# Three taps of a depthwise convolution moved from TensorE to VectorE

## The chip, the cores and the metric

One core of a Trainium2 chip runs the kernel. The metric is the time on the device in microseconds, the median of several runs. A profile is taken of one execution; its span is the time from the first to the last instruction.

## The reference, cut to what matters

The model is a block of 272 tokens (16 meta tokens and 256 of the sequence) and then two blocks of 256 tokens with a width of 1024. The second of the three holds the mixer that the change touches. Its input projection gives `u_val` and `u_gate` of 512 channels each, and queries, keys and values of 8 heads. The two parts are computed beside each other:

```python
def causal_depthwise_conv(x, w):          # y_t = sum_j w_j * x_{t-W+1+j}
    ...
def conformer_conv(u_val, u_gate, conv_w, ln_g, ln_b):
    z = u_val * jax.nn.sigmoid(u_gate)
    z = causal_depthwise_conv(z, conv_w)   # W = 31, 512 channels
    z = layernorm(z, ln_g, ln_b)           # over the 512 channels
    return jax.nn.silu(z)

def mixer_ab(h, w_in, conv_w, ln_g, ln_b, w_out):
    ...
    ya = conformer_conv(u_val, u_gate, conv_w, ln_g, ln_b)
    yb = moba_attention(...)               # 8 heads, 256 tokens
    return jnp.concatenate([ya, yb], axis=-1) @ w_out
```

Everything is float32. Each weight matrix is multiplied in three passes of a high and a low part.

## The kernel before

Activations lie with channels on the 128 partitions and tokens along the free dimension. Weights stream from HBM in 281 slabs of 128x1024 through four buffers. SyncE loads a slab (`raw`), ScalarE makes the high part (`whi`, L464), VectorE subtracts for the low part (`wlo`, L839), and TensorE does the three products (`three`, L1236 to L1238). A `column` makes 128 output channels out of one slab, 24 matmuls of 256 columns; a `row` adds one slab's part to eight accumulators. VectorE's `take` (L883) moves a finished column from PSUM to `proj`, scales it, and then does the split of the slab three places ahead.

The order of work is written out by hand. In the mixer of the second block each engine runs a loop over the steps u = 0 to 18, and each engine's list for a step is executed in order; engines meet at semaphores only. On TensorE (the last loop of the printed code) a step holds: scores and transposes (even u) or attention products (odd u); then a weight column, if u is in `IN2_STEP`, whose keys are 1, 2, 3, 4, 6, 7, 8, 10 and 11; then for u = 1 to 8 half a convolution block (`conv_half`, block (u-1)//2, first half at odd u, second at even u); then at u = 9 the sum for the layernorm mean (L1618), at u = 10 that for the variance (L1623). Steps 5 and 9 hold no column.

The convolution. The 512 channels are four blocks of 128 in the order `GLU_ORDER`, and each block is four groups of 32 channels. GpSimd multiplies value and gate into `zpad` (30 zeros in front) and issues DMAs that lay four versions of each group, shifted by 0 to 3 tokens, on the 4 x 32 partitions of `zsh`. One matmul with a 128x32 matrix of diagonals then adds four taps of one group; eight of these (q = 0 to 7, `CONV_Q`) make the 31 taps and one of weight zero. A block is 8 x 4 matmuls into one half of the PSUM bank `acc_bank[3]`, and a half block is 16. With the last one `conv_summed` is raised. ScalarE then copies the block from PSUM to `cv` (L711, at even u, the last thing of the step but the layernorm) and raises `conv`. TensorE's first half of block i waits for `conv` >= i, and the mean's matmuls wait for `conv` >= 4.

VectorE's list for an even step: `maxima` (bias and maximum of the scores, L1089 and L899), `take` and split. For an odd step: `normalized` (reciprocal L905 and two scalings L908, which wait for ScalarE's exponentials), then `take` and split, if the step has a column. At u = 9 it also subtracts the mean (L1114).

The parameters that are per channel are packed in one tensor `par` of 144 columns, which ScalarE's queue loads first in the kernel. The third block's mixer has a convolution of 4 taps whose last three are chained VectorE instructions (L1191), each with its weight out of `par`.

Of the kernel before, what the change touches and what calls it, by code (L numbers as in the profile page):

```python
# [27 lines left out]
ALU = mybir.AluOpType  # L28
ACT = mybir.ActivationFunctionType
# [4 lines left out]
KC = DM // P  # L34
SEQ = 256
# [11 lines left out]
CONV_T = 31  # L47
CONV_C = 4
SHIFTS = 4
CONV_Q = 8  # L50
CONV_X = SEQ + SHIFTS * (CONV_Q - 1)
LRU_T = 4
LRU_C = 8.0
# [35 lines left out]
def in1_lo(d):  # L89
# [16 lines left out]
GLU_ORDER = (0, 2, 1, 3)  # L106
# [31 lines left out]
PAR = (("norm1", KC), ("norm2", KC), ("final_norm", KC), ("mix_norm_2", 2 * KC), ("mlp_norm_2", 2 * KC),  # L138
       ("final_norm_2", KC), ("c_conv_b_2", KC), ("c_b_r_2", KC), ("c_b_i_2", KC), ("c_lambda_2", KC),
       ("pool_scale", 2), ("fox_out_gain", 3), ("sb_out_gain", 3), ("ab_ln_g_2", CONV_C), ("ab_ln_b_2", CONV_C),  # L140
       ("c_conv_w_2", LRU_T * KC))
COL = {name: sum(n for _, n in PAR[:i]) for i, (name, _) in enumerate(PAR)}
PAR_N = sum(n for _, n in PAR)
G_PROD = PAR_N
# [22 lines left out]
def build(nc, slabs, xT, par_in, fbias_in, poolw_in, gatew_in, convw_in, out):  # L167
    with ExitStack() as ctx:
# [8 lines left out]
        acc_bank = bank[2:6]  # L177
# [4 lines left out]
        def half(b, j):  # L182

            return b[:, SEQ * (j % 2):SEQ * (j % 2) + SEQ]
# [28 lines left out]
        par = sb("par", [P, PAR_N + KC])  # L213
# [21 lines left out]
        zpad = sb("zpad", [P, CONV_C, CONV_X + SHIFTS])  # L235
        t8 = sb("t8", [P, KC, SEQ])
        cv = t8[:, 0:CONV_C, :]
# [6 lines left out]
        zsh = shared[:, n_convw:n_convw + n_zsh].rearrange("p (k g x) -> p k g x", k=CONV_C, g=4)  # L244
# [52 lines left out]
        conv_summed, conv = sem("conv_summed"), sem("conv")  # L297
# [145 lines left out]
        def _(act):  # L443
# [111 lines left out]
            for i in range(PIECES):  # L555
                act.wait_ge(x_loaded[i], 16)
                for k in (2 * i, 2 * i + 1):
                    g = GAIN[N_NORM1] + k
# [120 lines left out]
            for i in range(len(IN2_FIRST)):  # L679
                split_ahead(IN2 + i)  # L680
                if i in (1, 3, 5, 7):
                    k = GLU_ORDER[i // 2]
# [4 lines left out]
            for u in range(MOBA_U + 3):  # L687
                if u in IN2_STEP or u in OUT2_STEP:
                    split_ahead(n)
                    n += 1  # L690
                if u == max(IN2_STEP) + 1:
                    act.wait_ge(slab_used, OUT2)
                    operand_hi(A_CAT2, F_CAT2, CAT2_STEP[u])
                if u % 2 == 0:
                    if 1 <= u // 2 <= MOBA_S:
                        transposed(u // 2 - 1, FOX_S, moba_copies)
                    if u % 4 == 0 and u < MOBA_U:
                        pair = u // 4
                        act.wait_ge(vT, 7 + pair)
                        act.activation(vtok[:, 0:2, P * pair:P * pair + P],  # L700
                                       acc_bank[2][:, 0:2 * P].rearrange("p (g d) -> p g d", g=2), ACT.Copy).then_inc(v_ready, 1)
                    if u // 2 < MOBA_S:
                        probabilities(u // 2, FOX_S, MOBA_N)
                if u >= 6 and u % 4 == 2:
                    pair = u // 4 - 1
                    act.wait_ge(o_ready, FOX_S + 2 * pair + 2)
                    act.activation(af[:, PAIR_CHUNK[pair], :], aux_bank[:, 0:SEQ], ACT.Copy).then_inc(af_ready, 1)
                if 2 <= u <= 2 * CONV_C and u % 2 == 0:
                    i = u // 2 - 1
                    act.wait_ge(conv_summed, i + 1)  # L710
                    act.activation(cv[:, GLU_ORDER[i], :], half(acc_bank[3], i), ACT.Copy).then_inc(conv, 1)  # L711
                if u == LN_MEAN_STEP:
                    for k in range(CONV_C):
                        act.wait_ge(ln_dev, k + 1)
                        act.activation(sq[:, k, NMETA:], cv[:, k, :], ACT.Square).then_inc(ln_sq, 1)
                if u == LN_VAR_STEP:
                    act.wait_ge(ln_var, 1)
                    inverse_root(r1[:, :], std[:, NMETA:], half(acc_bank[3], 1), CONV_C * P).then_inc(ln_std, 1)
                if u == MOBA_U:
                    for k in range(CONV_C):  # L720
                        g, b = COL["ab_ln_g_2"] + k, COL["ab_ln_b_2"] + k
                        act.wait_ge(ln_norm, k + 1)
                        act.activation(af[:, CONV_CHUNK + k, :], cv[:, k, :], ACT.Silu, scale=par[:, g:g + 1], bias=par[:, b:b + 1])\
                            .then_inc(af_ready, 1)
                if u in CAT2_STEP and u > max(IN2_STEP) + 1:
                    operand_hi(A_CAT2, F_CAT2, CAT2_STEP[u])
# [57 lines left out]
            for i in range(2 * KC):  # L784
                if IN3 + i < OUT3 - 1:
                    split_ahead(IN3 + i)
                if i < KC:
                    w, b = COL["c_conv_w_2"] + KC * (LRU_T - 1) + i, COL["c_conv_b_2"] + i
# [31 lines left out]
            for k in range(FINAL_D, KC):  # L820
                g = GAIN[N_FINAL] + k
# [5 lines left out]
        def _(dve):  # L827
# [95 lines left out]
            for i in range(PIECES):  # L923
                for b in range(2):
# [4 lines left out]
                    w = (slice(None), b, slice(2 * i, 2 * i + 2), slice(None))  # L929
# [41 lines left out]
            for u in range(ROW1_SLOT + KC):  # L971
# [10 lines left out]
                if u in SB_SCORES:  # L982
# [4 lines left out]
                    for hd in range(2):  # L987
                        ins = dve.tensor_tensor(sbz[p % 2][:, hd, :], sb_bank[hd][:, 0:SBW], sbneg[:, :], ALU.add)
# [7 lines left out]
                if u in SB_SUMS:  # L996
                    p = SB_SUMS[u]
                    dve.wait_ge(r_ready, p + 1)
                    for hd in range(2):
                        ins = dve.tensor_tensor(sbz[p % 2][:, hd, :], sbz[p % 2][:, hd, :], sb_bank[hd][:, 0:SBW], ALU.subtract)  # L1000
                    ins.then_inc(r_masked, 1)
                if u == 7:
                    dve.wait_ge(pool_mixed, 1)
                    for c in range(2):
                        g = COL["pool_scale"] + c
# [10 lines left out]
                if u == 6:  # L1016

                    dve.wait_ge(pool_d, 1)
                    for w, buf, p0, c in ((2, win, 0, 0), (4, win2, HD, 0), (8, win, 0, 1), (16, win2, HD, 1)):
                        ins = dve.scalar_tensor_tensor(pd[p0:p0 + HD, c, :], buf[p0:p0 + HD, c, NMETA:], 1.0 / w,  # L1020
                                                       proj[p0:p0 + HD, PU + c, NMETA:], ALU.mult, ALU.subtract)
# [70 lines left out]
            for u in range(MOBA_U + 3):  # L1092

                if u == max(IN2_STEP) + 1:
                    operand_lo(A_CAT2, CAT2_STEP[u])
                    split_ahead(OUT2 - 1)
                softmax_slot(u, MOBA_S, FOX_S, MOBA_N, alibi_bias)
                if u == LN_VAR_STEP + 1:
                    dve.wait_ge(ln_std, 1)
                    for k in range(CONV_C):  # L1100
                        dve.tensor_tensor(cv[:, k, :], cv[:, k, :], r1[:, :], ALU.mult).then_inc(ln_norm, 1)
                if u in IN2_STEP:
                    c = IN2_STEP[u]
                    take(n, acc_bank[n % 2], c, QSCALE if 8 <= c < 12 else 1.0, ahead=n < OUT2 - 1)
                    n += 1
                if u in OUT2_STEP:
                    split_ahead(n)
                    n += 1
                if u in CAT2_STEP and u > max(IN2_STEP) + 1:
                    operand_lo(A_CAT2, CAT2_STEP[u])  # L1110
                if u == LN_MEAN_STEP:
                    dve.wait_ge(ln_mean, 1)
                    for k in range(CONV_C):
                        dve.scalar_tensor_tensor(cv[:, k, :], half(acc_bank[3], 0), -1.0 / (CONV_C * P), cv[:, k, :],  # L1114
                                                 ALU.mult, ALU.add).then_inc(ln_dev, 1)
# [63 lines left out]
            for i, c in enumerate(IN3_ORDER):  # L1179
# [4 lines left out]
                if 1 <= i <= KC:  # L1184

                    k = i - 1
                    dve.wait_ge(tap0, k + 1)
                    for t in range(LRU_T - 1):
                        w = COL["c_conv_w_2"] + KC * t + k
                        x0 = NMETA - LRU_T + 1 + t  # L1190
                        ins = dve.scalar_tensor_tensor(af[:, k, :], proj[:, 8 + k, x0:x0 + SEQ], par[:, w:w + 1],  # L1191
                                                       af[:, k, :], ALU.mult, ALU.add)
# [26 lines left out]
            for k in range(FINAL_D):  # L1219
                g = GAIN[N_FINAL] + k  # L1220
                ins = dve.tensor_scalar(af[:, k, :], h[:, k, NMETA:], par[:, g:g + 1], None, ALU.mult)
# [10 lines left out]
        def _(pe):  # L1232
# [156 lines left out]
            for t in range(2):  # L1389
                ins = pe.transpose(aux_bank[:, FOX_HEADS * t:FOX_HEADS * t + FOX_HEADS],  # L1390
                                   cum[0:FOX_HEADS, NMETA + P * t:NMETA + P * t + P],
                                   ident[0:FOX_HEADS, 0:FOX_HEADS])
# [72 lines left out]
            for u in range(ROW1_SLOT + KC):  # L1465
# [13 lines left out]
                if u == 7:  # L1479
# [3 lines left out]
                    for g in range(4):  # L1483
                        b, c = HD * (g % 2), g // 2
                        ins = pe.matmul(aux_bank[b:b + HD, SEQ * c:SEQ * c + SEQ], poolw[b:b + HD, c, :],
                                        pd[b:b + HD, c, :], start=True, stop=True)
# [80 lines left out]
            def conv_half(i, part):  # L1567

                k = GLU_ORDER[i]
                if part == 0:  # L1570
                    pe.wait_ge(convw_loaded, 16 * CONV_C)
                    pe.wait_ge(z_shifted[i], 16 * 4 * SHIFTS)
                    if i >= 1:
                        pe.wait_ge(conv, i)
                for q in range(part * CONV_Q // 2, (part + 1) * CONV_Q // 2):
                    for g in range(4):
                        ins = pe.matmul(half(acc_bank[3], i)[32 * g:32 * g + 32, :], convw[:, k, g, q, :],  # L1577
                                        zsh[:, k, g, SHIFTS * q:SHIFTS * q + SEQ], start=(q == 0), stop=(q == CONV_Q - 1),
                                        skip_group_check=True)
                if part == 1:  # L1580
                    ins.then_inc(conv_summed, 1)
            for u in range(MOBA_U + 3):
# [32 lines left out]
                if u == LN_MEAN_STEP:  # L1615
                    pe.wait_ge(conv, CONV_C)
                    for k in range(CONV_C):
                        ins = pe.matmul(half(acc_bank[3], 0), ones[:, :], cv[:, k, :], start=(k == 0), stop=(k == CONV_C - 1))  # L1618
# [37 lines left out]
            for i in range(2, 2 * KC):  # L1656
# [3 lines left out]
                k = i - 2  # L1660
# [89 lines left out]
```

## Time and profile before

| what | value |
| --- | --- |
| median of 3 runs | 937.27 us (935.64 to 938.26) |
| profiled execution | 936.92 us, of it the span 935.2 us |
| TensorE matmul busy | 904.7 us, 97% |
| VectorE busy | 596.3 us, 64% |
| ScalarE busy | 465.3 us, 50% |
| GpSimd busy | 94.9 us, 10% |
| mean granted TensorE clock | 0.985 of full speed |

Busy time counts an engine's instructions, not its waits; matmuls overlap in the pipeline, so the sum of their durations is more than the time they take. The chain that ended last goes back from the last instruction to what released it, step by step. Times in the views are microseconds from the start of the span.

### The profile page before, as it was taken

What the parts mean: (1) busy time and instruction counts of PE and PEld (TensorE: products, weight loads), DVE (VectorE), ACT (ScalarE), POOL (GpSimd) and SP (SyncE); (2) the same over time, 40 slices, a digit from 0 to 9 for tenths busy, and PEclk for the clock granted to TensorE, in tenths of its full rate; (3) what the DMA queues carried; (4) which work ended last, traced back from release to release, by engine and by line L of the source; (5) the groups of instructions that cost most, each with busy time, mean ns of one, the idle gap of its engine ahead of it and who ended that gap; (6) DMA issues with size and microseconds to landing.
All of it is one profiled execution on the core that took longest, in us unless ns stands there. A gap on an engine that the chain in (4) does not pass through costs nothing.

```text
span 935.2 us, 19567 instructions
## 1 busy us (share of the span) xinstructions
PE 904.7 (97%) x7444; PEld 867.8 (93%) x7444; DVE 596.3 (64%) x967; ACT 465.3 (50%) x742; POOL 94.9 (10%) x149
## 2 busy tenths in 40 slices
PE   8989999999999999999999999999998999999997
PEld 8878888999999998977899999999898899999996
DVE  5765446665666577545585566666879975556665
ACT  6444456543444355534664444444777644444443
POOL 4220001100000004920010000000222100000000
PEclk9998889999999999999999999999999999999999
DMA  7432223756555654732536555555344455555551
GB/s 256 158 114 68 68 86 118 244 184 202 179 182 177 203 181 133 240 96 85 192 129 201 189 188 180 179 184 199 135 136 157 158 166 192 185 190 186 180 179 46
DMA packets 44947, 152.64 MB, mean 163 GB/s; under 512 B 5860, under 2 KB 7140, under 8 KB 44900
## 3 DMA queue, kind: packets, MB, share of 16 engines
q1 hardware_dynamic: 41184, 145.52, 47.3%
q0 software_dynamic: 2912, 5.48, 1.8%
q10 hardware_dynamic: 804, 0.98, 0.3%
q8 instruction: 34, 0.56, 0.3%
q14 instruction: 13, 0.11, 0.0%
HBM read 148.58 MB, written 1.05 MB: 160 GB/s over the span
## 4 chain that ended last, share of the span: by engine, by line
PE 88%; DVE 8%; ACT 2%; issue 1%; DMA 1%; SPq 0%; DVEq 0%; POOL 0%; ACTq 0%
PE bank L1236 26%; PE bank L1238 25%; PE bank L1237 25%; DVE alo L864 3%; PE bank L1446 2%; PE bank L1577 2%; DVE wlo L839 1%; PE bank L1326 1%; DVE h L874 1%; PE bank L1271 1%; PE bank L1343 1%; PE bank L1668 1%; PE bank L1366 1%; ACT whi L464 1%; DMA raw<-in_slabs 1%
## 5 line engine op out<-in xcount | busy, mean ns | idle before, releaser
L1236 PE MATMUL bank<-ahi,whi 128*128 128x256 f32 (+1 forms) x1400 | 404.3, 289 | 5.2 <-DVE proj L883 2.9
L1238 PE MATMUL bank<-ahi,wlo 128*128 128x256 f32 (+1 forms) x1400 | 396.4, 283 | 0.0
L1237 PE MATMUL bank<-alo,whi 128*128 128x256 f32 (+1 forms) x1400 | 396.2, 283 | 0.0
L839 DVE TENSOR_TENSOR wlo<-raw,whi 128x1024 fp32r<-128x1024 f32 x273 | 333.5, 1230 | 32.9 <-ACT whi L464 32.6
L464 ACT ACTIVATE whi<-raw 128x1024 fp32r<-128x1024 f32 x273 | 282.2, 1050 | 119.2 <-PE bank L1238 114.5
L1236 PEld LDWEIGHTS bank<-ahi,whi 128*128 128x128 f32 x1400 | 267.1, 191 | 9.5 <-DVE proj L883 3.5
L1237 PEld LDWEIGHTS bank<-alo,whi 128*128 128x128 f32 x1400 | 267.3, 191 | 0.5
L1238 PEld LDWEIGHTS bank<-ahi,wlo 128*128 128x128 f32 x1400 | 267.2, 191 | 0.0
L1236 PE MATMUL bank<-hidhi,whi 128*128 128x256 f32 x704 | 197.4, 280 | 3.2 <-issue 2.1
L1237 PE MATMUL bank<-hidlo,whi 128*128 128x256 f32 x704 | 196.9, 280 | 0.0
L1238 PE MATMUL bank<-hidhi,wlo 128*128 128x256 f32 x704 | 196.9, 280 | 0.0
L1236 PEld LDWEIGHTS bank<-hidhi,whi 128*128 128x128 f32 x704 | 132.4, 188 | 3.7 <-issue 3.4
L1237 PEld LDWEIGHTS bank<-hidlo,whi 128*128 128x128 f32 x704 | 132.5, 188 | 0.0
L1238 PEld LDWEIGHTS bank<-hidhi,wlo 128*128 128x128 f32 x704 | 132.3, 188 | 0.0
L1127 DVE SCALAR_TENSOR_TENSOR y<-bank,rstd 128x256 f32<-128x256 f32 x64 | 27.2, 424 | 123.2 <-PE bank L1238 121.2
L747 ACT ACTIVATE hidhi<-y 128x256 fp32r<-128x256 f32 x64 | 26.8, 418 | 133.3 <-DVE y L1127 130.1
L371 POOL TENSOR_TENSOR sq<-sq 128x256 f32<-128x256 f32 (+1 forms) x23 | 22.3, 996 | 521.5 <-ACT sq L491 345.6
L883 DVE SCALAR_TENSOR_TENSOR proj<-bank,rstd 128x256 f32<-128x256 f32 (+1 forms) x56 | 23.7, 427 | 61.1 <-PE bank L1238 59.2
L653 ACT ACTIVATE hidhi<-y 128x256 fp32r<-128x256 f32 x22 | 9.2, 418 | 60.9 <-DVE y L1043 60.9
L423 POOL DMA_DIRECT2D shared<-zpad x64 | 31.4, 499 | 1.3 <-POOL zpad L418 1.2
L1135 DVE TENSOR_TENSOR hidlo<-y,hidhi 128x256 fp32r<-128x256 f32 x64 | 27.2, 425 | 3.4 <-ACT hidhi L747 1.1
L864 DVE SCALAR_TENSOR_TENSOR alo<-h,par,ahi 128x256 fp32r<-128x256 f32 (+1 forms) x48 | 27.6, 639 | 0.0
(198 smaller groups left out, 719.2 us busy)
## 6 DMA issues: line engine op xcount, KB each, us to landing
raw<-in_slabs SPq DMA_DIRECT2D x273, 512.0 KB, 3.4
shared<-zpad POOLq DMA_DIRECT2D x64, 35.5 KB, 3.1
shared<-in_convw POOLq DMA_DIRECT2D x4, 512.0 KB, 6.3
raw<-in_slabs SPq DMA_DIRECT2D x8, 128.0 KB, 5.7
vtok<-in_gatew POOLq DMA_DIRECT2D x2, 512.0 KB, 4.3
out<-y SPq DMA_DIRECT2D x4, 256.0 KB, 2.7
h<-in_xT ACTq DMA_DIRECT2D x3, 272.0 KB, 5.4
h<-in_xT SPq DMA_DIRECT2D x1, 272.0 KB, 3.4
```

What stands on the lines that cost most here:

```text
L371: pool.tensor_tensor(t8[:, j, :] if i == N_MIX0 else a, a, b, ALU.add).then_inc(sum_ready, 1)
L423: pool.dma_start(zsh[32 * s:32 * s + 32, k, g, :], zpad[32 * g:32 * g + 32, k, s:s + CONV_X])\
L464: act.activation(whi[:, n % R, :, :], raw[:, n % R, :, :], ACT.Copy).then_inc(hi_done, 1)
L747: act.activation(hidhi[:, hid_buf(f, FF2 - 1), :], hid[:, f % 2, :], ACT.Square).then_inc(hid_hi, 1)
L839: dve.tensor_tensor(wlo[:, n % R, :, :], raw[:, n % R, :, :], whi[:, n % R, :, :].bitcast(F32), ALU.subtract).then_inc(lo_done, 1)
L864: dve.scalar_tensor_tensor(alo[:, k, lo:], h[:, k, lo:], par[:, g:g + 1], ahi[:, k, lo:].bitcast(F32), ALU.mult, ALU.subtract).then_inc(al ...
L883: dve.scalar_tensor_tensor(proj[:, d, lo:], src[:, lo:T1], scale, rstd[:, lo:], ALU.mult, ALU.mult).then_inc(gemm_evac, 1)
L1127: dve.scalar_tensor_tensor(hid[:, f % 2, :], col_bank(f)[:, NMETA:T1], 0.0, rstd[:, NMETA:], ALU.max, ALU.mult).then_inc(gemm_evac, 1)
L1135: dve.tensor_tensor(hidlo[:, b, :], hid2[:, f % 2, :], hidhi[:, b, :].bitcast(F32), ALU.subtract).then_inc(hid_lo, 1)
L1236: pe.matmul(dst, hi, xh, start=start, stop=False, skip_group_check=True)
L1237: pe.matmul(dst, hi, xl, start=False, stop=False, skip_group_check=True)
L1238: return pe.matmul(dst, lo, xh, start=False, stop=stop, skip_group_check=True)
```

## The change

The last tap group (q = 7, taps 28 to 30) is no longer computed by TensorE, in all four blocks. ScalarE's copy of the block out of PSUM is removed. In its place VectorE adds the three taps in three chained instructions, in the step after (u = 3, 5, 7, 9, behind `normalized` and ahead of `take`): the first reads the block's sum out of PSUM, multiplies the shifted `zpad` with the tap's weight, adds, and writes `cv`; the two others add to `cv` in place. With the last one `conv` is raised. The weights of all taps are appended to `par`, which grows from 144 to 268 columns.

```diff
+CONV_PE = CONV_Q - 1
...
-       ("c_conv_w_2", LRU_T * KC))
+       ("c_conv_w_2", LRU_T * KC), ("ab_conv_w_2", CONV_T * CONV_C))
...
-                if 2 <= u <= 2 * CONV_C and u % 2 == 0:
-                    i = u // 2 - 1
-                    act.wait_ge(conv_summed, i + 1)
-                    act.activation(cv[:, GLU_ORDER[i], :], half(acc_bank[3], i), ACT.Copy).then_inc(conv, 1)
...
+                if 3 <= u <= 2 * CONV_C + 1 and u % 2 == 1:
+                    i = u // 2 - 1
+                    k = GLU_ORDER[i]
+                    dve.wait_ge(conv_summed, i + 1)
+                    for t in range(SHIFTS * CONV_PE, CONV_T):
+                        w = COL["ab_conv_w_2"] + CONV_C * t + k
+                        src = half(acc_bank[3], i) if t == SHIFTS * CONV_PE else cv[:, k, :]
+                        ins = dve.scalar_tensor_tensor(cv[:, k, :], zpad[:, k, t:t + SEQ], par[:, w:w + 1], src, ALU.mult, ALU.add)
+                        if t < CONV_T - 1:
+                            link(ins)
+                    ins.then_inc(conv, 1)
...
                 if u == LN_MEAN_STEP:
                     dve.wait_ge(ln_mean, 1)
+                    dve.wait_ge(conv, CONV_C)
...
-                for q in range(part * CONV_Q // 2, (part + 1) * CONV_Q // 2):
+                for q in range(0, CONV_Q // 2) if part == 0 else range(CONV_Q // 2, CONV_PE):
...
-                                        ... start=(q == 0), stop=(q == CONV_Q - 1),
+                                        ... start=(q == 0), stop=(q == CONV_PE - 1),
```

## Rows read from the trace of the kernel before

**Rows 1.** The page: busy time by engine; the chain that ended last, by line.

```profile
PE 904.7 (97%) x7444; PEld 867.8 (93%) x7444; DVE 596.3 (64%) x967; ACT 465.3 (50%) x742; POOL 94.9 (10%) x149
...
PE bank L1236 26%; PE bank L1238 25%; PE bank L1237 25%; DVE alo L864 3%; PE bank L1446 2%; PE bank L1577 2%; DVE wlo L839 1%; PE bank L1326 1%; DVE h L874 1%; PE bank L1271 1%; PE bank L1343 1%; PE bank L1668 1%; PE bank L1366 1%; ACT whi L464 1%; DMA raw<-in_slabs 1%
```

**Rows 2.** Busy time by stretch: length, engines (instructions), clock, DMA share, GB/s.

```profile
388.00:434.00 46.00, 45.48 (x503) 34.52 (x503) 21.89 (x54) 16.67 (x41) 14.48 (x29) 1.00 0.42 128
```

**Rows 3.** The chain in 408 to 434 us: start, length, what.

```profile
409.30 1.86 PE bank L1577 x32
411.16 0.59 PE bank L1366 x8
411.76 1.94 PE bank L1577 x32
...
422.79 1.86 PE bank L1577 x32
...
428.71 1.86 PE bank L1577 x32
430.58 0.59 PE bank L1366 x8
431.16 1.92 PE bank L1618 x8
```

**Rows 4.** VectorE in time: start, length, line, operation, count, idle before it.

```profile
398.49 1.21 DVE L839 TENSOR_TENSOR wlo<-raw,whi 128x1024 fp32r<-128x1024 f32 x1
...
409.34 0.42 DVE L883 SCALAR_TENSOR_TENSOR proj<-bank,rstd 128x256 f32<-128x256 f32 x1 [2.75 <-PE bank L1238]
409.68 1.22 DVE L839 TENSOR_TENSOR wlo<-raw,whi 128x1024 fp32r<-128x1024 f32 x1
410.81 0.16 DVE L905 RECIPROCAL rinv<-rsum 128x2 f32<-128x2 f32 x1
411.01 0.48 DVE L908 TENSOR_SCALAR prob<-prob,rinv 128x128 f32<-128x128 f32 x2
...
419.23 0.62 DVE L908 TENSOR_SCALAR prob<-prob,rinv 128x256 f32<-128x256 f32 x2
...
430.42 0.48 DVE L908 TENSOR_SCALAR prob<-prob,rinv 128x128 f32<-128x128 f32 x2
```

**Rows 5.** ScalarE in time: the second of the four copies.

```profile
411.23 0.38 ACT L711 ACTIVATE t<-bank 128x256 f32<-128x256 f32 x1 [3.31 <-PE bank L1577]
```

**Rows 6.** The later mixer's taps: durations; two trios and a GpSimd multiplication in time.

```profile
L1191 DVE SCALAR_TENSOR_TENSOR af<-proj,par,af x24: 476/485/914, 667.2 to 694.3; 128x256 f32<-128x256 f32 x24
...
667.20 1.52 DVE L1191 SCALAR_TENSOR_TENSOR af<-proj,par,af 128x256 f32<-128x256 f32 x3 [0.34 <-ACT af L790]
...
677.98 1.95 DVE L1191 SCALAR_TENSOR_TENSOR af<-proj,par,af 128x256 f32<-128x256 f32 x3
...
678.39 0.74 POOL L433 TENSOR_TENSOR y<-y,af 128x256 f32<-128x256 f32 x1 [2.94 <-ACT y L773]
```

**Rows 7.** VectorE in time: four unchained instructions that read PSUM.

```profile
433.13 1.42 DVE L1114 SCALAR_TENSOR_TENSOR t<-bank,t 128x256 f32<-128x256 f32 x4 [2.22 <-PE bank L1618]
```

**Rows 8.** The chain where TensorE goes on after the long wait.

```profile
456.63 0.44 DVE alo L858
457.12 0.39 PE bank L1236
```

**Rows 9.** The start: parameter load, ScalarE's first use, chain, GB/s by slice.

```profile
par<-in_par ACTq DMA_DIRECT2D x1, 72.0 KB, 3.6
...
5.39 0.93 ACT L559 ACTIVATE ahi<-h,par 128x272 fp32r<-128x272 f32 x2
...
2.68 5.99 DMA raw<-in_slabs
...
GB/s 256 158 114 68 68 86 118 244 184 202 179 182 177 203 181 133 240 96 85 192 129 201 189 188 180 179 184 199 135 136 157 158 166 192 185 190 186 180 179 46
```

**Rows 10.** GpSimd in time: the last block's DMA issues.

```profile
394.94 7.85 POOL L423 DMA_DIRECT2D shared<-zpad  x16 [0.29 <-POOL zpad L418]
```

More of the change, by code:

```diff
@@ L1574, in conv_half @@
                         pe.wait_ge(conv, i)
-                for q in range(part * CONV_Q // 2, (part + 1) * CONV_Q // 2):
+                for q in range(0, CONV_Q // 2) if part == 0 else range(CONV_Q // 2, CONV_PE):
                     for g in range(4):
                         ins = pe.matmul(half(acc_bank[3], i)[32 * g:32 * g + 32, :], convw[:, k, g, q, :],
-                                        zsh[:, k, g, SHIFTS * q:SHIFTS * q + SEQ], start=(q == 0), stop=(q == CONV_Q - 1),
+                                        zsh[:, k, g, SHIFTS * q:SHIFTS * q + SEQ], start=(q == 0), stop=(q == CONV_PE - 1),
                                         skip_group_check=True)
```

## The prediction

> **What bounds the kernel now.** I read the page's busy times and the chain that ended last first. TensorE is busy 97% of the span, and the chain runs mostly over its matmuls; the convolution's matmuls (L1577) alone are 2% of the span [rows 1]. Then I read the stretch that holds the convolution, 388 to 434 us: PE 45.48 of 46.00 us busy, VectorE only 21.89, ScalarE 16.67, granted clock 1.00, which is the 2.4 GHz level [rows 2]. So whatever leaves TensorE here shortens the run, and whatever TensorE is made to wait for lengthens it; VectorE has half its time free, but what counts is where in TensorE's order it is late. The third view is the chain through this stretch piece by piece. The eight half-convolutions are on it in full, 1.86 us each (16 matmuls). Behind the half of step 4 come only attention products (0.59 us) and then at once the next block's first half at 411.76; behind the half of step 8 come 0.59 us of products and then at once the layernorm-mean matmuls at 431.16. At the two other joints (the one at 422.79 is shown) a whole weight column of about 3 us lies between [rows 3]. The fourth view is VectorE's order in time, to see when it would reach the taps [rows 4].
>
> **The change part by part.**
>
> TensorE. Each block loses one of eight tap groups, 4 matmuls. A half of 16 takes 1.86 us (its 32 records are two for each matmul), so one matmul is 0.116 us and four are 0.466 us. Over four blocks 1.86 us leave the path, always in the block's second half, at steps 2, 4, 6 and 8. If nothing else moved, that would be the gain.
>
> ScalarE. Four copies leave. They wait on TensorE and last 0.38 us; the one at 411.23 ends 411.61, before TensorE has finished its products at 411.76 [rows 3, 5]. They cost TensorE nothing today, so their removal gives nothing. ScalarE's splits behind them can begin earlier, but VectorE's half of each split waits behind its own take, so no slab is ready sooner: zero.
>
> VectorE. Per block three chained instructions: one reads PSUM and the shifted input, two read SBUF twice, each with a per-partition weight. The trace has the same form and size in the later mixer: L1191, three chained taps, 1.52 us for the three, 476 to 914 ns each [rows 6]. For the PSUM one there is no such row with a per-partition scalar. Bounds for the trio: four unchained instructions of this kind out of PSUM took 1.42 us, 0.36 us each, which makes 1.07 us for three; a slow group of L1191 took 1.95 us [rows 6, 7]. I take 1.52 us, the row that has the chain and the scalar.
>
> In VectorE's order the trio stands in the odd step behind `normalized`, that is behind take, weight split, reciprocal and two scalings of the even step. Let T be the end of the column of the even step, when TensorE begins the second half.
> - Step 5 (T = 409.30): take 409.34, split 409.68, reciprocal 410.81, scalings 411.01 to 411.49 [rows 4]. Instructions here overlap by 0.08 us (take 409.34 + 0.42 against split 409.68), so the trio starts at 411.41 and ends at 412.93. TensorE picks up 0.05 us after VectorE's last write, as after the operand that ends at 457.07 [rows 8]: 412.98. TensorE itself would be ready at 409.30 + 1.40 + 0.59 = 411.29. It stands idle 1.7 us. Against the 411.76 of today this block's first half begins 1.22 us later.
> - Step 9 (T = 428.71): scalings end 430.90, trio 430.82 to 432.34, TensorE 432.39, against 431.16 today: 1.23 us later.
> - Steps 3 and 7: the scalings end at 419.85 in step 7, trio until 421.3, and TensorE needs it at 422.79 less the savings before it [rows 3, 4]. Hidden with about 1 us to spare; step 3 has the same order and the same column between. A trio of 1.95 us would still fit.
>
> So the savings at steps 4 and 8 lie inside the two new stalls, and only those at steps 2 and 6 are real: 1.22 + 1.23 - 0.466 - 0.466 = +1.52 us. With 1.07 us for the trio it is +0.6, with 1.95 us +2.4. What waits behind the trio on VectorE: in step 5 nothing until the scores of step 6, in step 9 the deviations, which themselves wait for the mean that TensorE sums late; ScalarE's squares wait for those. All of these hang on TensorE's time and move with it, as does the chain over ScalarE and VectorE that holds TensorE up until 457.12 [rows 8]. I find nothing later that would absorb the shift, since the following stages run in TensorE's order at 97% busy.
>
> A rule speaks for less. The Trainium skill, VectorE: DVE Perf Modes, section "The DRAIN you can't avoid", holds that a semaphore after each VectorE instruction costs nothing beyond the drain that comes anyway. By it the trio would go at the unchained pitch, 1.07 us, and the sum would be +0.6 us in place of +1.5. The chained row, 1.52 us for three, disagrees, and I go by the row.
>
> The parameter load. The packed parameters grow by 31 x 4 = 124 columns, 128 x 124 x 4 bytes = 63.5 KB on top of 72 KB. The load is issued before the others and landed about 3.6 us after its issue; ScalarE's first use is at 5.39 us, so a somewhat later landing is itself covered. But the chain at the start runs over the raw weight pieces, in flight until 8.67 us, and the extra bytes share the same engines: at 256 GB/s (first slice of the page) 63.5 KB are 0.25 us [rows 9]. Bounds: 0 (the pieces are held by latency and not bytes) and 0.5. I take 0.25.
>
> Sum: +1.52 + 0.25 = +1.8 us. The profiled execution took 936.92 us (span 935.2 and 1.7 around it), which gives 938.7; it stands 0.35 us below the median of the runs, so against the median 937.27 it is 939.0 us.
>
> **The rivals.**
>
> 1. The stalls don't come and the removed matmuls count in full: -1.86 + 0.25 = -1.6 us, 935.7. This needs the trio done by 411.29 and 430.7, for instance with the scalings earlier than today. VectorE's 24 us of free time in the stretch speak for it [rows 2]; against it stands that the scalings, which come before the trio in program order, alone end at 411.49 [rows 4]. Half way, with the trio at 1.07 us, lies the no-change case.
>
> 2. The delay is made and then absorbed, or the start costs nothing and the trio is short: 0 to +0.6 us, 937.3 to 937.9. Against it: no slack in which to absorb it is seen behind 434 us.
>
> 3. Clearly slower: each tap is slowed by GpSimd, as where L1191 reached 914 ns. Three taps at 914 ns are 2.74 us, so each of the two stalls grows by 1.22: +1.8 + 2.4 = +4.2 us, 941.5. It decides from a trio of about 2.0 us on (then +2.8 us). For it: in the later mixer three taps took 1.95 us from 677.98 on, with a GpSimd multiplication at 678.39 beside them [rows 6]. Against: in the stretch here POOL only issues DMAs, from 394.94 until 402.79, and is idle at both joints; a VectorE split with two SBUF inputs inside that time, at 398.49, took 1.21 us as the one outside, at 409.68, took 1.22 [rows 4, 10]. The Trainium skill, SBUF — State Buffer, section "Who interferes with whom", says that a VectorE instruction with two SBUF inputs blocks against a GpSimd one that reads SBUF, for the whole instruction; the 1.95 us beside GpSimd's multiplication agree, and by the rule only block 0's taps could be touched here.
>
> **How the numbers follow.** Forecast with its own range 938.2 to 940.1 (trio 1.07 to 1.95, start 0 to 0.5): 0.66. Rival 1: 0.09. Rival 2: 0.13. Rival 3 and costs of its size that I don't see (a new placement in SBUF behind the longer parameter tile, a further wait): 0.12. Runs of one kernel differ by 2.6 us (935.64 to 938.26), and a median can lie 1 us off, which widens it: 936.7 to 941.2. About 0.3%, 2.8 us, is what a measurement tells from no change: slower means above 940.1, faster below 934.5. From the cases: slower 0.17, faster 0.04, same 0.79.
>
> **What would show each step.** In the profile of the changed kernel: halves of 1.86 us followed by halves of 1.40; a trio of about 1.5 us on VectorE starting right behind the scalings; two idle gaps of TensorE of about 1.7 us that end with the last tap, at the first half of the third block and at the mean's matmuls, and none at the second and fourth block; first weight pieces landing some 0.25 us later. No gap at these two joints would make the prediction wrong towards faster; a trio of over 2 us, or a gap at a third place, towards slower.

## The result and the profile after

The changed kernel takes 939.1 us in the median of 18 runs (936.24 to 940.97), the kernel before 936.12 us in the median of 18 (934.07 to 938.61) taken beside it. The medians lie 3.0 us apart, the means (938.68 and 936.45 us) 2.2 us. The ratio over all runs is 1.0023 with a 95% interval of 1.0012 to 1.0034: slower by 2.2 us (1.1 to 3.2). That is a real loss, and the estimate lies under the 0.3% at which it was to be called more than no change.

In the stretch that holds the convolution, the busy time has moved as the diff says. The columns are length, then busy time (instructions) of PE, PEld, DVE, ACT and POOL, granted clock, DMA share and GB/s; it answers to [rows 2]:

```profile
388.00:434.00 46.00, 42.09 (x462) 32.42 (x462) 26.47 (x63) 15.06 (x35) 14.66 (x29) 1.00 0.40 127
```

TensorE is now busy 42.1 of the 46 us instead of 45.5. Less work for it and yet a longer run: it must be waiting. The view of TensorE's waits from 386 to 465 us names them (who waits, for whom, us in total, times, longest). The last three lines were there before; the first two are new:

```profile
PE bank L1587 <- DVE t L1107: 1.7, 1, 1.7
PE bank L1628 <- DVE t L1107: 1.7, 1, 1.7
PE bank L1246 <- DVE alo L855: 1.6, 1, 1.6
PE bank L1353 <- DVE proj L880: 0.5, 1, 0.5
PE bank L1376 <- ACT probT L550: 0.5, 1, 0.5
```

L1587 is the convolution's matmul (L1577 before), L1628 the sum for the layernorm mean (L1618 before), L1107 the taps. The chain of the changed kernel through step 5, which answers to [rows 3], shows what the path consists of now:

```profile
408.88 0.42 DVE proj L880
409.30 1.13 DVE wlo L836
410.55 0.48 DVE prob L905 x2
411.03 0.40 DVE t L1107
411.45 0.50 DVE t L1107
411.97 0.50 DVE t L1107
412.47 0.14 issue
412.61 1.93 PE bank L1587 x32
```

Take, weight split, scalings, three taps: all of VectorE's list stands on the path where before the chain went over TensorE's matmuls. The block's first half begins at 412.61 and not at 411.76. At the mean's sum it is the same (432.78, before 431.16):

```profile
431.29 0.40 DVE t L1107
431.71 0.50 DVE t L1107
432.24 0.50 DVE t L1107
432.78 1.99 PE bank L1628 x8
```

To compare kernels I use one stretch, from the first score matmuls to the place where TensorE goes on behind the convolution's output. In the kernel before it runs from this row to the 457.12 of [rows 8], 68.37 us:

```profile
388.75 0.49 PE L1343 MATMUL bank<-proj 64*128 64x128 f32 x4 [0.52 <-DVE proj L883]
```

In the changed kernel it runs from 388.75 to 458.84, 70.09 us:

```profile
388.75 0.49 PE L1353 MATMUL bank<-proj 64*128 64x128 f32 x4 [0.52 <-DVE proj L880]
...
458.84 0.39 PE L1246 MATMUL bank<-ahi,whi 128*128 128x256 f32 x1 [1.57 <-DVE alo L855]
```

That is +1.72 us in one profiled execution of each. The spans differ by 2.2 us (937.4 and 935.2); the other 0.5 us arises later, in code that is the same in both. From the first of the eight residual adds behind this mixer to the first of the last eight, the kernel before takes 450.7 us and the changed one 451.2.

With the kernels of the eight experiments below this makes two groups. The kernel before and four others (parameters only, blocks 1 and 3, two more instructions, columns moved without the taps) take 450.7 to 450.8 us; the changed kernel and the other four take 451.1 to 451.3. The granted clock sorts them in the same way: from 460 to 932 us it is 1.00 in the first group, and in the second it falls once, near 720 us. Here are 720 to 730 us of the kernel before, and then of the changed one:

```profile
720.00:730.00 10.00, 9.87 (x80) 9.41 (x79) 9.80 (x18) 4.42 (x7) 0.00 (x0) 1.00 0.57 182
```

```profile
720.00:730.00 10.00, 10.00 (x75) 10.00 (x74) 9.77 (x17) 5.27 (x8) 0.00 (x0) 0.83 0.49 165
```

In the 8 us in front of the fall in the changed kernel TensorE was busy 5.89 us, and in the same 8 us of work in the kernel before (710 to 718 us) 5.89 too. So the 0.5 us goes with a fall of the clock and isn't work of the taps: two of the kernels without it have the taps of steps 5 and 9 on VectorE. What makes the clock fall there in some executions stays open.

### The profile page after: what moved, and what is told of

Read it like the earlier page. It is cut to its first block, busy times and chain, and to the rows that moved or that the text cites. A ratio compares the mean times of both kernels' runs of the same rounds, so it can differ in the third digit from the quotient of the medians.

```text
span 937.4 us, 19512 instructions
## 1 busy us (share of the span) xinstructions
PE 903.6 (96%) x7412; PEld 868.0 (93%) x7412; DVE 602.2 (64%) x979; ACT 464.9 (50%) x738; POOL 95.1 (10%) x149
## 4 chain that ended last, share of the span: by engine, by line
PE 88%; DVE 8%; ACT 2%; issue 1%; DMA 1%; SPq 0%; DVEq 0%; POOL 0%; ACTq 0%
PE bank L1246 26%; PE bank L1248 26%; PE bank L1247 26%; DVE alo L861 3%; PE bank L1456 2%; DVE wlo L836 1%; PE bank L1336 1%; PE bank L1587 1%; DVE h L871 1%; PE bank L1281 1%; PE bank L1353 1%; PE bank L1678 1%; DMA raw<-in_slabs 1%; PE bank L1376 1%; ACT whi L465 1%
```

## The experiments

The stretch is read from one profiled execution of each kernel; the granted clock is 1.00 in it (386 to 460 us) in all ten. A ratio is that of the runs of this kernel to runs of the kernel before taken beside them, with its 95% interval. "Theory A" is that of the prediction.

**Parameters only.**

```diff
-       ("c_conv_w_2", LRU_T * KC))
+       ("c_conv_w_2", LRU_T * KC), ("ab_conv_w_2", CONV_T * CONV_C))
```

> The kernel before with only the parameter tensor widened from 144 to 268 columns. Theory A (the loss is two waits of TensorE for the last tap, at steps 5 and 9): the stretch from the first scores (388.75 in the trace before) to TensorE's restart (457.12) stays at 68.4 us, and the total moves by 0 to 0.25 us. Rival B (the longer load or the new placement of everything behind the parameter tile costs): the total moves by most of the 2 us, with no new wait at steps 5 and 9.

Measured: ratio 0.999 (0.9976 to 1.0003), stretch 387.55 to 455.89, 68.34 us. The load is 134 KB instead of 72 and lands 3.8 us after its issue, here and in the changed kernel, and 3.6 before, but the first weight products that the start's chain waits for begin at the same time. The chain at the start, of this kernel:

```profile
2.68 6.00 DMA raw<-in_slabs
...
12.61 1.27 PE bank L1264 x8
```

Before it was 5.99 us [rows 9] and also 12.61. The larger load costs nothing that can be seen, and neither does the new placement of the tiles behind it. Rival B in this form falls. The 68.34 us beside the 68.37 of the kernel before also tell how well the stretch repeats.

**Only blocks 0 and 2, only blocks 1 and 3.** A function `on_dve(i)` chooses the blocks; the others keep eight tap groups and ScalarE's copy.

```diff
+def on_dve(i):
+    return i % 2 == 0        # the other kernel: i % 2 == 1
...
+                if 2 <= u <= 2 * CONV_C and u % 2 == 0 and not on_dve(u // 2 - 1):
...                              # ScalarE's copy as before
-                if 3 <= u <= 2 * CONV_C + 1 and u % 2 == 1:
+                if 3 <= u <= 2 * CONV_C + 1 and u % 2 == 1 and on_dve(u // 2 - 1):
...                              # TensorE: eight groups where not on_dve(i)
```

> Only blocks 0 and 2 get their last three taps on VectorE (steps 3 and 7); blocks 1 and 3 stay as in the kernel before. Theory A: both trios are hidden behind a weight column, both savings of 0.47 us count, so the stretch from the first scores to the restart is 67.4 us (0.93 shorter than 68.4) and no wait for a tap is seen. Rival B (VectorE's added work costs wherever it stands): half of the loss, 69.2 us.

> Only blocks 1 and 3 get their taps on VectorE (steps 5 and 9). Theory A: both savings lie inside the waits, which remain in full, 1.7 us each; the stretch is 68.4 + 1.72 + 0.93 = 71.0 us, slower than with all four blocks though half the taps are moved. Rival B: half of the loss, 69.2 us.

Measured with blocks 0 and 2: stretch 388.73 to 456.23, 67.50 us, that is 0.87 shorter than before, and TensorE waits for no tap; ratio 0.999 (0.9973 to 1.0008), which by itself doesn't separate it from no change. With blocks 1 and 3: stretch 387.35 to 458.33, 70.98 us; ratio 1.0032 (1.0019 to 1.0046). Its two new waits of TensorE:

```profile
PE bank L1598 <- DVE t L1117: 1.7, 1, 1.7
PE bank L1639 <- DVE t L1117: 1.7, 1, 1.7
```

The same instructions, the same count of them, in one pair of places a gain and in the other a loss of 2.6 us. Rival B, 69.2 us for each, falls: what the trio costs here depends on where TensorE uses it. The two add up: -0.87 + 2.61 = +1.74, and both together cost 1.72.

**The taps ahead of the scalings.** The block of the diff is put in front of `softmax_slot(...)` in VectorE's step.

```diff
+                if 3 <= u <= 2 * CONV_C + 1 and u % 2 == 1:
+                    ...                          # the block of the diff
                 softmax_slot(u, MOBA_S, FOX_S, MOBA_N, alibi_bias)
```

> The changed kernel with the trio ahead of the reciprocal and scalings in VectorE's odd step instead of behind them. Theory A: the trio starts when the weight split ends, 0.6 us earlier, so each of the two waits shrinks from 1.7 to about 1.1 us and the stretch is 68.9 us (70.1 less 2 x 0.6). Rival C (the scalings, now 1.5 us later, hold the next step's transposes up): a new wait of TensorE for the scaled probabilities, and the stretch stays at 70 us or more.

Measured: stretch 385.61 to 454.46, 68.85 us; ratio 0.9997 (0.9982 to 1.0013). The waits of this kernel from 386 to 465 us, in which the scaled probabilities don't appear (the 0.5 us ahead of the first scores ends at 385.61, outside the window):

```profile
PE bank L1246 <- DVE alo L855: 1.6, 1, 1.6
PE bank L1587 <- DVE t L1102: 1.2, 1, 1.2
PE bank L1628 <- DVE t L1102: 1.1, 1, 1.1
PE bank L1376 <- ACT probT L550: 0.5, 1, 0.5
```

Rival C falls. The scalings ahead of the taps made 0.6 us of each wait. The rest is the list still in front, take and weight split, and the trio itself. The stretch is still 0.5 us longer than before, and the ratio can't tell that from no change.

**The taps left out.** Seven tap groups, ScalarE's copy as before, nothing added.

```diff
-                for q in range(part * CONV_Q // 2, (part + 1) * CONV_Q // 2):
+                for q in range(0, CONV_Q // 2) if part == 0 else range(CONV_Q // 2, CONV_PE):
...                              # stop at q == CONV_PE - 1
```

> The kernel before with taps 28 to 30 left out and not added anywhere; ScalarE's copy stays. Theory A: the savings count in full, 4 x 0.466 us, and the stretch from the first scores to the restart is 66.5 us (68.4 less 1.86). Rival D (part of the removed matmul time was never on the path): less than 1.4 us shorter.

Measured: stretch 387.52 to 454.11, 66.59 us, 1.78 shorter; ratio 0.9984 (0.9969 to 1.0). The savings are real and nearly the 1.86 us worked out, and rival D falls; this rests on the stretch, as the interval of the ratio reaches 1.0. Taken away from the +1.72, the waits cost 3.5 us.

**Two more instructions in each trio.**

```diff
+                    for _ in range(2):
+                        link(ins)
+                        ins = dve.scalar_tensor_tensor(cv[:, k, :], zpad[:, k, CONV_T:CONV_T + SEQ], 0.0, cv[:, k, :], ALU.mult, ALU.add)
                     ins.then_inc(conv, 1)
```

> The changed kernel with two more chained VectorE instructions per block that add zero times the shifted input, 0.5 us each. Theory A: every added microsecond on VectorE at steps 5 and 9 is a microsecond of TensorE's wait, and none at steps 3 and 7: each wait 2.7 us, the stretch 70.1 + 2 x 1.0 = 72.1 us. Rival B (VectorE's work costs wherever it stands): four times 1.0, 74.1 us.

Measured: stretch 389.40 to 461.49, 72.09 us; ratio 1.0058 (1.0039 to 1.0077). Its waits:

```profile
PE bank L1590 <- DVE t L1112: 2.7, 1, 2.7
PE bank L1631 <- DVE t L1112: 2.6, 1, 2.6
```

The two instructions make VectorE's list 0.9 us longer in each block, 3.7 us in all, and 2.0 arrive in the stretch: 0.9 at each of steps 5 and 9, and 0.1 at each of steps 3 and 7. There the five just fail to fit: TensorE's half block begins 0.02 to 0.05 us later than in the changed kernel, and takes 1.93 us instead of 1.86. Rival B, 74.1 us, falls.

**The columns moved, with and without the taps.** If the cause is that no column stands in front of TensorE's use at steps 5 and 9, then a column there must bring the gain. The same diff on the changed kernel and on the kernel before:

```diff
-IN2_STEP = {1: 9, 2: 13, 3: 17, 4: 10, 6: 14, 7: 18, 8: 11, 10: 15, 11: 19}
+IN2_STEP = {1: 9, 2: 13, 3: 17, 5: 10, 6: 14, 7: 18, 9: 11, 10: 15, 11: 19}
```

> The changed kernel with the weight columns of steps 4 and 8 moved to steps 5 and 9, so that each step in which TensorE needs the trio's result has a column of about 2.8 us in front of it. Theory A: no wait for a tap is left, all four savings of 0.47 us count, the stretch is 66.5 us (1.86 under the kernel before), and the total about 934.5 to 935.3 us. Rival E (the moved columns open another wait, at the even steps that lose theirs, for example for the scaled probabilities or the copies out of PSUM): a new wait of TensorE, stretch 67.5 us or more.

> The kernel before with only the same two columns moved, taps and copies as before. Theory A: the copies were hidden already, so nothing is gained, 68.4 us, and all of the gain of the previous kernel comes from the taps. Rival F (the move itself gains or loses): the stretch differs by over 0.3 us from 68.4.

Measured with the taps on VectorE: 935.18 us, ratio to the kernel before 0.9982 (0.9967 to 0.9996), stretch 388.74 to 455.48, 66.74 us. The control without them: ratio 1.0001 (0.9986 to 1.0015), stretch 388.76 to 457.20, 68.44 us. Rival E, with 67.5 us or more, and rival F, with over 0.3 us for the move alone, fall. The waits of the kernel with taps, from 384 to 463 us, are the three old ones only:

```profile
PE bank L1246 <- DVE alo L855: 1.6, 1, 1.6
PE bank L1353 <- DVE proj L880: 0.5, 1, 0.5
PE bank L1376 <- ACT probT L550: 0.5, 1, 0.5
```

VectorE in time at step 5 of that kernel. The trio now ends at 409.61, TensorE's half block begins at 411.07, and VectorE itself waits in between (the bracket of the last line):

```profile
407.49 0.17 DVE L902 RECIPROCAL rinv<-rsum 128x2 f32<-128x2 f32 x1 [1.36 <-ACT prob L528]
407.69 0.48 DVE L905 TENSOR_SCALAR prob<-prob,rinv 128x128 f32<-128x128 f32 x2
408.09 0.48 DVE L1107 SCALAR_TENSOR_TENSOR t<-zpad,par,bank 128x256 f32<-128x256 f32 x1
408.60 1.01 DVE L1107 SCALAR_TENSOR_TENSOR t<-zpad,par,t 128x256 f32<-128x256 f32 x2
411.10 0.42 DVE L880 SCALAR_TENSOR_TENSOR proj<-bank,rstd 128x256 f32<-128x256 f32 x1 [1.50 <-PE bank L1248]
```

The move changes VectorE's side too: the column's take and weight split now stand behind the trio and no longer in front. Which of the two brings the gain? TensorE at step 4 and 5 of this kernel (second half, products, column), and the second half in the changed kernel:

```profile
405.94 1.50 PE L1587 MATMUL bank<-shared 128*32 128x256 f32 x24
407.37 0.66 PE L1376 MATMUL bank<-probT,vtok 128*64 128x128 f32 x8
407.96 0.39 PE L1246 MATMUL bank<-ahi,whi 128*128 128x256 f32 x1
```

```profile
408.77 1.50 PE L1587 MATMUL bank<-shared 128*32 128x256 f32 x24
```

Counted from there the trio ends no earlier than it did, 3.7 us later in both (409.61 and 412.45), because the reciprocal ahead of it now waits 1.36 us for ScalarE's exponentials. Without a column TensorE would have stood idle from about 408.0 to 409.6, nearly as long as the 1.7 us before (an estimate from these rows). So the column in front of TensorE's use brings the gain.

The move by itself is worth nothing, the taps by themselves lose 2.2 us, and both together gain 1.7 us (0.4 to 3.1) on the kernel before. Of the kernels that compute all of the reference this one has the shortest stretch, 66.74 us against 67.50 with blocks 0 and 2. Its median is the lowest of them too, but the intervals of the ratios overlap.

## Why the prediction was right

The mechanism is the one forecast, and in the stretch its size too: +1.72 us where +1.52 was worked out. That the median, 939.1 us, is the forecast's 939.0 is luck. The forecast added 1.8 us to a median of 937.27; the kernel before measured 936.12 beside the changed one, and the medians differ by 3.0. The profiled executions differ by 2.2 us of span: the start's 0.25 didn't come, the stretch gave 0.2 more, and 0.5 came with a fall of the clock that the forecast doesn't have. The lower end of its range, 938.2, doesn't follow from its own bounds either: 937.27 with +0.6 and a start of 0 is 937.9.

1. Removed matmuls, 1.86 us off the path if nothing else moved: shown, 1.78 with the taps left out. The halves of the second kind took 1.43 us in the changed kernel's chain, against 1.40 worked out.
2. ScalarE's copies free: agrees, no step shows a gain from their removal; it was not tested alone.
3. The trio at 1.52 us, from the chained row and not at the unchained pitch: shown. Chained, it runs from 410.94 to 412.45 in the changed kernel's step 5. The parts are these, and the first, out of PSUM, is no dearer than the others:

```profile
410.94 0.47 DVE L1107 SCALAR_TENSOR_TENSOR t<-zpad,par,bank 128x256 f32<-128x256 f32 x1
411.45 1.00 DVE L1107 SCALAR_TENSOR_TENSOR t<-zpad,par,t 128x256 f32<-128x256 f32 x2
```

   The distance from one start to the next is 0.51 us, while the unchained four of [rows 7], which have no per-partition weight, have 0.34 (1.42 less one of 0.41, over three). Two rows separate the chain from the weight. The first is the kernel with two more instructions, chained and without a per-partition weight, 0.43 us each. The second is the kernel before at its start, unchained and with a per-partition weight, 0.49 us each on 272 columns:

```profile
413.26 0.88 DVE L1112 SCALAR_TENSOR_TENSOR t<-zpad,t 128x256 f32<-128x256 f32 x2
```

```profile
12.48 0.90 DVE L864 SCALAR_TENSOR_TENSOR alo<-h,par,ahi 128x272 fp32r<-128x272 f32 x2
```

   Start to start that is 0.46 us chained (0.34 unchained) without the weight, and 0.41 us unchained (0.51 chained) with it. So the chain makes 0.10 to 0.12 us of the 0.17 for each instruction, and the weight the rest; the operands of these rows don't lie in the same memories, and the split is an estimate to that degree. The Trainium skill, under "The DRAIN you can't avoid" in VectorE: DVE Perf Modes, has it that a semaphore after each instruction costs nothing extra. By the prediction's use of it the stretch would have come out at +0.6 us; +1.72 was measured, and these rows disagree with it as well.
4. Waits of 1.7 us at steps 5 and 9, none at 3 and 7: shown to 0.1 us in the changed kernel, and by both half changes.
5. The sum for the stretch, +1.52: measured +1.72. The term that was too small is TensorE's pick-up behind the wait. I took 0.05 us from [rows 8]; at step 5 it is 0.14 us (the "issue" line), and the sum behind the second wait takes 1.99 us where it took 1.92. That is 0.16 of the 0.20 us; the rest isn't placed.
6. The parameter load, +0.25: wrong. Its bytes didn't lengthen the flight of the weight pieces, 6.00 us against 5.99, and neither does the changed kernel begin its first weight products more than 0.03 us later (12.64); of the bounds that stood there, 0 was true.
7. Rival 1 (no waits, -1.6 us) became true only where the columns were moved for it. Rival 3 (taps slowed by GpSimd) didn't occur: block 0's trio, which ran while GpSimd issued DMAs, took no longer than the others. Rival 2 (the delay absorbed) fell with the interval of the ratio and with the last residual add, which the profiled execution of the changed kernel reaches 2.2 us later; 1.7 of these are there already at the first add behind the mixer (472.94 us, before 471.22).

## What to carry to other kernels

Moving work from a full engine to one that is half idle pays by the place and not by the idle share: write out, at each use of the moved result, the consumer's time to get there and the producer's list up to it. Here two of four uses had a weight column of 3 us in front, and two had 0.6 us of products. The column left room for about 0.9 us more than the trio: with that much added the fit just failed. When the list comes out late, look for other work that the consumer may do first; two keys in an order table turned a loss of 2.2 us into a gain of 1.7. A saving that lies just ahead of such a wait is lost in it and must not be counted.

## What the runs showed of the hardware

I had not expected where the spread between executions comes from. The kernel with the taps ahead of the scalings reached the first scores at 385.61, the kernel before at 388.75, although the code up to there differs only in the parameter load. The load isn't the reason, as the kernel with parameters only, which has the same one, reached them at 387.55. The stretch 120 to 156 us of the kernel before, and then of that one:

```profile
120.00:156.00 36.00, 35.30 (x259) 32.63 (x258) 19.21 (x28) 21.31 (x37) 0.00 (x0) 0.91 0.35 114
```

```profile
120.00:156.00 36.00, 35.06 (x279) 32.38 (x276) 22.09 (x37) 23.56 (x44) 0.00 (x0) 1.00 0.40 132
```

The first has a granted clock of 0.91, so a part of it ran at the lower level of 1.2 GHz, with 259 matmul records; the second is at 2.4 GHz throughout, with 279. If the rest of the first ran at 2.4 GHz, its mean of 0.91 makes some 6.5 us at half speed, which costs about 3.2 us (an estimate from this row); the landmark moved by 3.1. Ahead of it, at 100 to 120 us, the clock was 0.83 in both, with TensorE busy 19.70 of the 20 us. Not every difference is told by it: the kernel with two more instructions has, to two digits, the same granted clocks as the kernel before up to there and reached the first scores 0.65 us later, which stays open. A difference of 3 us is larger than the effect under study. For effects this small a stretch between two instructions of the same trace, at full clock, separates kernels that the medians of ten runs don't.
